# An inverse root moved from VectorE to ScalarE, and one chunk's VectorE order written out by itself

## The chip, the core and the metric

The program runs on one core of a Trainium2 chip. TensorE (PE) multiplies matrices, VectorE (DVE) and ScalarE (ACT) work element by element, GpSimd (POOL) does element-wise work on SBUF, and SyncE (SP) issues the transfers. Each engine takes its own instructions in the order in which they are written and waits at semaphores for the others. The metric is the device time of one execution in microseconds (us); lower is better.

## The reference

One layer of a hybrid encoder on 1,024 tokens of width 1,024, all in float32. What matters here is the second of its three token mixers (the SSD mixer) and the gated feed-forward part:

```python
# SSD mixer, after its scan: a gated norm over two groups of 192 channels
hg = (y.reshape(b_, s_, SSD_WIDTH) * jax.nn.silu(z.astype(jnp.float32)))
hg = hg.reshape(b_, s_, SSD_GROUPS, SSD_WIDTH // SSD_GROUPS)
hg = hg * lax.rsqrt(jnp.mean(jnp.square(hg), axis=-1, keepdims=True) + RMS_EPS)
ssd_out = (hg.reshape(b_, s_, SSD_WIDTH) * norm_w).astype(xbc.dtype)
...
mix = jnp.concatenate([pool_out, ssd_out, sb_out], axis=-1) @ w_out[i]
x = layer_norm(DEEPNORM_ALPHA * x + mix, ln1_g[i], ln1_b[i])
...
# feed-forward: up projection, causal convolution of width 3, gate, down projection
up = causal_depthwise_conv(x @ w_up, conv_w, conv_b)
gate, val = up[..., :D_FF], up[..., D_FF:]
ffn = (jax.nn.silu(gate) * val) @ w_down
```

## The kernel before, in words

**Numbers in two parts.** Every float32 matrix product is made as three matmuls on a high and a low part of each operand (`three`: high by high, high by low, low by high). ScalarE makes the high part by a rounding copy (`hi` for a whole weight unit of 128x1024, `op_hi` for a half of 128x512), VectorE the low part by a subtraction of the high part (`lo`, `op_lo`). A unit arrives by a transfer into one of two raw buffers; SP issues the transfer of a unit only when the low part of the unit two places earlier is made, since both share a buffer.

**The output projection.** The eight row blocks of `w_out` (units `("out", k)`) are taken in the order `OUT_ORDER = [5, 6, 7, 0, 1, 3, 2, 4]`. Blocks 2, 3 and 4 multiply the SSD mixer's result. TensorE sums the squares of the gated result (task `rm0`), then multiplies blocks 5, 6, 7, 0 and 1 for the first two token tiles, then spreads the inverse root over the partitions by two small products (tasks `sp0` and `sp2`, which read `tmp`), and then multiplies blocks 3, 2 and 4, each as 12 matmuls for the two token tiles. For each of these three blocks VectorE scales the mixer's tile (`normalised(k)`), ScalarE copies it to its high part, VectorE makes the low part of the weight block (`lo`) and then that of the tile (`mix_lo(k)`), and TensorE waits for that. In the kernel before, ScalarE makes the high part of a weight block ahead of the copy of the same step. The inverse root itself is: mean plus epsilon on VectorE, `Sqrt` on ScalarE, two reciprocals of half a tile on VectorE.

**The up projection.** It runs in 11 chunks of two column pairs; a pair (c, pp) is computed by a seven-product scheme after Strassen, with products named `A11, S1, S2, S3, A12, S4, A22` in TensorE's order, each of 12 matmuls. The operands `S1` to `S4` are sums of weight quarters that GpSimd makes in `weight_sums`; it can start when both raw buffers of the pair have arrived. The transfer into the second of them (`raw_b`) is issued by SP when VectorE has made the low part of `A22` of the pair before, and GpSimd's third sum waits for VectorE's low part of `S1`. VectorE adds products up in five steps, `combine(c, pp, 1)` to `combine(c, pp, 5)`; TensorE's `S4` product waits for step 2 and its `A22` product for step 3. VectorE also makes the convolution (`taps`), the gate product (`glu`) and the low part of the result (`h_low`), for whose high part ScalarE copies (`h_high`).

VectorE's order is written by hand: `first_chunk` for the first half of chunk 0 and `second_half(0)` for its second half, `chunk(c)` for the others, which calls `second_half(c)` too. After chunk 0 follow steps 1 and 2 of `combine(1, 0, ...)`.

Of the kernel before, what the change touches and what calls it, by code (L numbers as in the profile page):

```python
# [23 lines left out]
ALU = mybir.AluOpType  # L24
ACT = mybir.ActivationFunctionType

P = 128
D = 1024
S = 1024
HALF = 512  # L30
# [4 lines left out]
SSD_W = 384  # L35
# [11 lines left out]
RMS_EPS = 1e-6  # L47
# [24 lines left out]
OUT_ORDER = [5, 6, 7, 0, 1, 3, 2, 4]  # L72
# [5 lines left out]
UNIT = {u: n for n, u in enumerate(UNITS)}  # L78
# [215 lines left out]
def build(nc, ctx, a, out):  # L294
# [4 lines left out]
    def put(name, shape, dt=F32, at=None):  # L299

        size = -(-4 * int(np.prod(shape[1:])) // 32) * 32
        if at is None:
            at = top[0]
            top[0] += size
        assert at + size <= 229368, (name, at, size)
        return nc.alloc_sbuf_tensor_at(name, shape, dt, offset=at)

    def sem(name):
        return ctx.enter_context(nc.semaphore(name))
# [7 lines left out]
    un_b = put("weights_t1", [P, HALF], F32, top[0] - 4 * HALF)  # L317
    mask_r = put("mask", [P, P], F32R)
    zero = put("zero", [P, 1])
    cap_gt = put("cap_gt", [P, P])  # L320
    ident_r = put("ident_r", [P, P], F32R)
    pool_w = put("pool_w", [P, 2, P])
# [125 lines left out]
    xdt_done = sem("xdt_done")  # L448
    xw_done = sem("xw_done")
    hg_done, sq_done, nrm_done = sem("hg_done"), sem("sq_done"), sem("nrm_done")  # L450
    var_done, sqrt_done = sem("var_done"), sem("sqrt_done")
    rms_done = sem("rms_done")
    mixh = sem("mix_hi_done")
    ssd_split = sem("ssd_split")
# [64 lines left out]
    def hi(n):  # L519

        if UNITS[n][0] == "x":
            nc.scalar.wait_ge(x_raw[UNITS[n][1]], 16)
        else:
            nc.scalar.wait_ge(raw_in[raw_place(n) % RAWS], 16 * (raw_place(n) // RAWS + 1))
        wait_ring_free(nc.scalar, n)
        nc.scalar.activation(unit_place(n, False), unit_raw(n), ACT.Copy).then_inc(hi_done, 1)

    def lo(n, eng=nc.vector):

        eng.wait_ge(hi_done, n + 1)  # L530
        eng.tensor_tensor(unit_place(n, True), unit_raw(n), unit_place(n, False).bitcast(F32),
                                ALU.subtract).then_inc(split_done, 1)
# [66 lines left out]
    def op_lo(c, o, pp, it=0):  # L599

        nc.vector.wait_ge(op_hi_done, lo_count(c, o, pp) + 18 * it)
        nc.vector.tensor_tensor(op_place(c, o, pp, True), op_raw(c, o, pp), op_place(c, o, pp, False).bitcast(F32),  # L602
                                ALU.subtract).then_inc(op_lo_done, 1)
# [634 lines left out]
    def _(eng):  # L1238
# [208 lines left out]
        pooled_high(1)  # L1447
        squared(2)
        hi(UNIT[("out", 7)])
        nc.scalar.preload_act_table(ACT.Sqrt)  # L1450
        for k in (0, 1):
            hi(UNIT[("out", k)])
        eng.wait_ge(var_done, 1)
        act(tmp[:, :], tmp[:, :], ACT.Sqrt).then_inc(sqrt_done, 1)
        for k, unit in enumerate(OUT_ORDER[5:]):
            hi(UNIT[("out", unit)])
            i = (1, 0, 2)[k]
            eng.wait_ge(nrm_done, k + 1)
            act(mh[:, 2 + i, :], cv[:, i, :], ACT.Copy).then_inc(mixh, 1)


        def gain_bias(m):
# [171 lines left out]
    def _(eng):  # L1634
# [3 lines left out]
        def link(ins):  # L1638

            chained[0] += 1  # L1640
            ins.then_inc(dve_chain, 1)
            eng.wait_ge(dve_chain, chained[0])
# [33 lines left out]


        link(v.memset(zero[:, :], 0.0))
        for i, (n, s_) in enumerate(FIRST):
            if i < 3:  # L1680
                eng.wait_ge(first_hi, i + 1)
            else:
                eng.wait_ge(hi_done, 2)
            ins = v.tensor_tensor(unit_place(n, True)[:, s_], unit_raw(n)[:, s_], unit_place(n, False)[:, s_].bitcast(F32),  # L1684
                                  ALU.subtract)
            if i < 3:
                ins.then_inc(first_lo, 1)
            else:
                ins.then_inc(split_done, 2)
# [69 lines left out]
        def task(name):  # L1759
            eng.wait_ge(d_full, TASKS.index(name) + 1)  # L1760
            pair = task_place(name)[0]
            return two(pair), d_free[pair]
# [69 lines left out]
        def normalised(k):  # L1832
            i = (1, 0, 2)[k]
            src = task("sp%d" % i)[0] if k else tmp[:, :]
            v.scalar_tensor_tensor(out=cv[:, i, :], in0=cv[:, i, :], scalar=param("norm_w", i), in1=src,
                                   op0=ALU.mult, op1=ALU.mult).then_inc(nrm_done, 1)
# [5 lines left out]
                            ALU.subtract).then_inc(ssd_split, 1)  # L1842

        lo(UNIT[("out", 0)])
        src, free = task("rm0")
        v.tensor_scalar(tmp[:, :], src, 1.0 / (SSD_W // 2), RMS_EPS, ALU.mult, ALU.add).then_inc(var_done, 1)
        lo(UNIT[("out", 1)])
        eng.wait_ge(sqrt_done, 1)
        for h in range(2):
            s_ = slice(h * HALF, (h + 1) * HALF)  # L1850
            v.reciprocal(tmp[:, s_], tmp[:, s_]).then_inc(rms_done, 1)
        eng.wait_ge(rms_done, 2)
        normalised(0)
        lo(UNIT[("out", OUT_ORDER[5])])
        mix_lo(0)
        normalised(1)
# [72 lines left out]
        def taps(c, pp, r, it=0, parts=(1, 2)):  # L1929

            t = 2 * pp + r
            src = up_row(pp, r)
            w = PARAMS["ff_w"] + 3 * (4 * c + t)
            if 1 in parts:
                eng.wait_ge(row_tap, 4 * c + t + 1 + 4 * it)
                v.scalar_tensor_tensor(out=cf[:, r, 1:], in0=src[:, :S - 1], scalar=column(w + 1, 12, it),  # L1936
                                       in1=cf[:, r, 1:], op0=ALU.mult, op1=ALU.add).then_inc(row_mid, 1)
            if 2 in parts:
                eng.wait_ge(row_mid, 4 * c + t + 1 + 4 * it)
                v.scalar_tensor_tensor(out=cf[:, r, 2:], in0=src[:, :S - 2], scalar=column(w, 12, it),  # L1940
                                       in1=cf[:, r, 2:], op0=ALU.mult, op1=ALU.add).then_inc(row_done, 1)

        def glu(c, pp, it=0):

            eng.wait_ge(silu_ff, 2 * c + pp + 1 + 2 * it)
            eng.wait_ge(row_done, 4 * c + 2 * pp + 2 + 4 * it)
            v.tensor_tensor(cf[:, 0, :], cf[:, 0, :], cf[:, 1, :], ALU.mult).then_inc(glu_done, 1)
# [49 lines left out]
        def first_chunk():  # L1997

            combine(0, 0, 1)
            combine(0, 0, 2)  # L2000
            for i in range(2):
                eng.wait_ge(t_hi, 14 + 2 * i)
                v.tensor_tensor(t4l[:, 2 * i:2 * i + 2, :], sum_4[i][:, :, :], t4h[:, 2 * i:2 * i + 2, :].bitcast(F32),
                                ALU.subtract).then_inc(t_lo, 2)
            combine(0, 0, 3)
            op_lo(0, A22, 0)
            op_lo(0, A11, 1)
            combine(0, 0, 4)
            taps(0, 0, 0, 0, (1,))
            op_lo(0, S1, 1)  # L2010
            taps(0, 0, 0, 0, (2,))
            op_lo(0, S2, 1)
            op_lo(0, S3, 1)
            op_lo(0, A12, 1)
            combine(0, 0, 5)
            op_lo(0, S4, 1)

        def second_half(c, it=0):

            taps(c, 0, 1, it)  # L2020
            op_lo(c, A22, 1, it)
            glu(c, 0, it)
            h_low(c, 0, it)
            op_lo(c + 1, A11, 0, it)
            combine(c, 1, 1, it)
            combine(c, 1, 2, it)
            op_lo(c + 1, S1, 0, it)
            combine(c, 1, 3, it)
            op_lo(c + 1, S2, 0, it)
            op_lo(c + 1, S3, 0, it)  # L2030
            combine(c, 1, 4, it)
            op_lo(c + 1, A12, 0, it)
            taps(c, 1, 0, it)
            combine(c, 1, 5, it)
            op_lo(c + 1, S4, 0, it)
            taps(c, 1, 1, it)
            if c + 1 < LASTC:
                op_lo(c + 1, D0A, 0, it)
            glu(c, 1, it)
            if c + 1 < LASTC:  # L2040
                op_lo(c + 1, D1A, 0, it)
            h_low(c, 1, it)

        def chunk(c, it=0):

            combine(c, 0, 1, it)
            combine(c, 0, 2, it)
            op_lo(c, D0B, 0, it)
            combine(c, 0, 3, it)
            op_lo(c, D1B, 0, it)  # L2050
            op_lo(c, A22, 0, it)
            combine(c, 0, 4, it)
            taps(c, 0, 0, it)
            add_down(c, range(5), it)
            op_lo(c, A11, 1, it)
            add_down(c, range(5, 8), it)
            op_lo(c, S1, 1, it)
            op_lo(c, S2, 1, it)
            add_down(c, range(8, 16), it)
            op_lo(c, S3, 1, it)  # L2060
            op_lo(c, A12, 1, it)
            combine(c, 0, 5, it)
            op_lo(c, S4, 1, it)
            second_half(c, it)

        first_chunk()
# [282 lines left out]
```

## Time and profile before

| what | value |
|---|---|
| median of 3 executions | 1308.34 us (1306.91 to 1311.1) |
| the profiled execution, its own time | 1305.79 us |
| its span, first to last instruction | 1304.0 us |
| TensorE busy | 1278.3 us (98%) |
| VectorE, ScalarE, GpSimd busy | 65%, 39%, 18% |
| mean granted TensorE clock | 0.997 |

Times in the rows below count from the first instruction of the profiled execution. An engine's busy time says little by itself; what decides is where TensorE stands idle, and for whom it then waits.

### The profile page before, as it was taken

To read this page: it belongs to the slowest core of one execution; us is meant where nothing else is said; L and a number is where in the kernel's file an instruction comes from. 1 tells how busy PE (TensorE), PEld (TensorE's weight loads), DVE (VectorE), ACT (ScalarE), POOL (GpSimd) and SP (SyncE) were. 2 spreads that over 40 slices of the span, in tenths; PEclk is the share of its full clock that TensorE was granted. 3 is DMA by queue.
4 is the path that set the end of the run, shared out by engine and by line. 5 is a ranking of instruction groups with operands and counts; after the bars stand their busy time and mean duration, and the time that the engine had idled before them with its cause. 6 is when DMAs were issued, how large, how long until landed. Compare 5 with 4: busy or idle time off the path is not lost.

```text
span 1304.0 us, 16439 instructions
## 1 busy us (share of the span) xinstructions
PE 1278.3 (98%) x6120; PEld 1013.1 (78%) x6120; DVE 847.0 (65%) x1006; ACT 513.2 (39%) x792; POOL 232.7 (18%) x157
## 2 busy tenths in 40 slices
PE   7999999999999999999899999999999999999997
PEld 6777777777876888888788787878787787888886
DVE  5546646646498447525777676768676768677864
ACT  5435545457664126113434242423242323233441
POOL 0000000062300003510311111111111121212117
PEclk9999999999999999999999999999999999999999
DMA  6101101000004122100121111111121102011113
GB/s 239 50 32 38 40 21 49 32 34 17 1 17 145 50 81 81 58 24 23 59 65 49 49 49 48 64 32 64 48 66 47 64 32 64 32 65 33 59 60 124
DMA packets 22804, 71.94 MB, mean 55 GB/s; under 512 B 2528, under 2 KB 2784, under 8 KB 22752
## 3 DMA queue, kind: packets, MB, share of 16 engines
q1 hardware_dynamic: 22752, 71.22, 15.9%
q8 instruction: 36, 0.59, 0.2%
q14 instruction: 16, 0.13, 0.0%
HBM read 67.02 MB, written 4.19 MB: 55 GB/s over the span
## 4 chain that ended last, share of the span: by engine, by line
PE 73%; DVE 9%; issue 2%; ACT 2%; DMA 2%; DVEq 0%; SPq 0%; ACTq 0%
PE ps L734 12%; PE ps L736 12%; PE ps L735 12%; PE ps L1093 9%; PE ps L1095 9%; PE ps L1094 9%; PE ps L812 1%; PE ps L829 1%; DVE conv_ff L1936 1%; PE ps L788 1%; ACT conv_ff L1513 1%; DMA down_raw<-u_down 1%; DVE w_lo L602 1%; PE ps L1131 1%; PE ps L1133 1%
## 5 line engine op out<-in xcount | busy, mean ns | idle before, releaser
L734 PE MATMUL ps<-x_hi,w_hi 128*128 128x512 f32 x336 | 140.0, 417 | 8.1 <-DVE x_lo L1684 7.1
L1093 PE MATMUL ps<-mix_hi,w_hi 128*128 128x512 f32 x352 | 140.0, 398 | 3.3 <-DVE partial L1967 3.3
L1095 PE MATMUL ps<-mix_hi,w_lo 128*128 128x512 f32 x352 | 139.9, 397 | 0.0
L1094 PE MATMUL ps<-mix_lo,w_hi 128*128 128x512 f32 x352 | 139.7, 397 | 0.0
L736 PE MATMUL ps<-x_hi,w_lo 128*128 128x512 f32 x336 | 133.2, 396 | 0.0
L735 PE MATMUL ps<-x_lo,w_hi 128*128 128x512 f32 x336 | 133.2, 396 | 0.0
L1988 DVE TENSOR_TENSOR acc<-acc,ps 128x512 f32<-128x512 f32 x144 | 96.0, 684 | 54.3 <-PE ps L736 53.3
L2241 POOL TENSOR_TENSOR weight_sums<-raw 128x512 f32<-128x512 f32 x22 | 32.1, 1457 | 483.2 <-DMA raw<-u_up 483.2
L734 PE MATMUL ps<-h_hi,w_hi 128*128 128x512 f32 x288 | 114.7, 398 | 1.5 <-DVE acc L1988 1.5
L736 PE MATMUL ps<-h_hi,w_lo 128*128 128x512 f32 x288 | 113.9, 396 | 0.0
L735 PE MATMUL ps<-h_lo,w_hi 128*128 128x512 f32 x288 | 113.9, 395 | 0.0
L597 ACT ACTIVATE w_hi<-weight_sums 128x512 fp32r<-128x512 f32 x44 | 27.8, 632 | 210.7 <-PE ps L736 161.9
L1094 PE MATMUL ps<-t_lo,w_hi 128*128 128x512 f32 x264 | 104.4, 396 | 0.0
L1095 PE MATMUL ps<-t_hi,w_lo 128*128 128x512 f32 x264 | 104.4, 396 | 0.0
L1093 PE MATMUL ps<-t_hi,w_hi 128*128 128x512 f32 x264 | 104.4, 395 | 0.0
L1513 ACT ACTIVATE conv_ff<-ps,params 128x1024 f32<-128x1024 f32 x44 | 53.0, 1205 | 90.7 <-DVE ps L1974 53.5
L1708 DVE TENSOR_TENSOR_SCAN ps<-ps,zero 128x1024 f32<-128x1024 f32 (+7 forms) x48 | 65.3, 1361 | 33.4 <-ACT ps L1297 33.3
L734 PEld LDWEIGHTS ps<-x_hi,w_hi 128*128 128x128 f32 x336 | 63.7, 189 | 24.3 <-DVE x_lo L1684 7.1
L1093 PEld LDWEIGHTS ps<-mix_hi,w_hi 128*128 128x128 f32 x352 | 66.5, 189 | 19.7 <-DVE partial L1967 3.7
L1094 PEld LDWEIGHTS ps<-mix_lo,w_hi 128*128 128x128 f32 x352 | 66.6, 189 | 16.1
L1095 PEld LDWEIGHTS ps<-mix_hi,w_lo 128*128 128x128 f32 x352 | 66.5, 189 | 16.1
L1936 DVE SCALAR_TENSOR_TENSOR conv_ff<-ps,params,conv_ff 128x1023 f32<-128x1023 f32 x44 | 56.4, 1281 | 33.0 <-ACT conv_ff L1513 32.9
(268 smaller groups left out, 2733.5 us busy)
## 6 DMA issues: line engine op xcount, KB each, us to landing
raw<-u_up SPq DMA_DIRECT2D x44, 512.0 KB, 3.3
raw<-u_in SPq DMA_DIRECT2D x22, 512.0 KB, 3.3
down_raw<-u_down SPq DMA_DIRECT2D x38, 256.0 KB, 2.8
x_stage<-u_x SPq DMA_DIRECT2D x8, 512.0 KB, 7.8
raw<-u_out SPq DMA_DIRECT2D x8, 512.0 KB, 3.3
x_nat<-x_nat SPq DMA_DIRECT2D x8, 512.0 KB, 3.2
raw<-u_gate SPq DMA_DIRECT2D x8, 512.0 KB, 3.2
out<-o_norm SPq DMA_DIRECT2D x7, 512.0 KB, 2.6
```

The costliest lines, as they stand in the source:

```text
L597: nc.scalar.activation(op_place(c, o, pp, False), op_raw(c, o, pp), ACT.Copy).then_inc(op_hi_done, 1)
L734: mm(dst, w_hi, x_hi, start=first, stop=False)
L735: mm(dst, w_hi, x_lo, start=False, stop=False)
L736: return mm(dst, w_lo, x_hi, start=False, stop=last)
L1093: mm(dst, w_h[:, k], t_h[:, kt, :], start=fresh and kt == 0, stop=False, skip_group_check=True)
L1094: mm(dst, w_h[:, k], t_l[:, kt, :], start=False, stop=False, skip_group_check=True)
L1095: last = mm(dst, w_l[:, k], t_h[:, kt, :], start=False, stop=kt == 3, skip_group_check=True)
L1513: act(cf[:, r, :], up_row(pp, r), ACT.Identity, scale=column(w, 12, it), bias=column(b, 4, it)).then_inc(row_tap, 1)
L1708: link(v.tensor_tensor_scan(z[:, ::-1], z[:, ::-1], zero[:, 0:1].broadcast_to([P, keys]), 1.0, ALU.mult, ALU.add))
L1936: v.scalar_tensor_tensor(out=cf[:, r, 1:], in0=src[:, :S - 1], scalar=column(w + 1, 12, it), in1=cf[:, r, 1:], op0=ALU.mult, op1=ALU.add). ...
L1988: v.tensor_tensor(dst, dst, ps[:, DOWN_BANKS[k % 4], :], ALU.add).then_inc(dn_added, 1)
L2241: g.tensor_tensor(t0[:, :], wb[:, 0:HALF], wb[:, HALF:D], ALU.add).then_inc(sum_done, 1)
```

## The change

The inverse root is computed on ScalarE, as the exponential of minus half a logarithm: one `Ln` of a whole tile that also takes the mean and the epsilon (a new constant tile), and two `Exp` of half a tile. VectorE's three instructions for it go, and so does the semaphore `sqrt_done`. The load of the square root's table comes after the two `Exp`. ScalarE makes the high parts of the weight blocks 3, 2 and 4 one place later: that of block 3 after the copy of step 0, that of block 2 after the copy of step 1, that of block 4 after the copy of step 2. VectorE makes the low part of block 1 after `normalised(0)`.

In the feed-forward part the nine calls at the head of `second_half` move out of it: into `chunk` as they were, and into `first_chunk` in another order, in which the first three steps of `combine(0, 1, ...)` come earlier and the low parts of `A22`, of the result and of the next pair's `A11` and `S1` later.

```diff
@@ -317,6 +317,7 @@
     un_b = put("weights_t1", [P, HALF], F32, top[0] - 4 * HALF)
     mask_r = put("mask", [P, P], F32R)
     zero = put("zero", [P, 1])
+    rms_eps = put("rms_eps", [P, 1])
     cap_gt = put("cap_gt", [P, P])
     ident_r = put("ident_r", [P, P], F32R)
     pool_w = put("pool_w", [P, 2, P])
@@ -448,7 +449,7 @@
     xdt_done = sem("xdt_done")
     xw_done = sem("xw_done")
     hg_done, sq_done, nrm_done = sem("hg_done"), sem("sq_done"), sem("nrm_done")
-    var_done, sqrt_done = sem("var_done"), sem("sqrt_done")
+    var_done = sem("var_done")
     rms_done = sem("rms_done")
     mixh = sem("mix_hi_done")
     ssd_split = sem("ssd_split")
@@ -1447,16 +1448,21 @@
         pooled_high(1)
         squared(2)
         hi(UNIT[("out", 7)])
+        src, _ = task("rm0")
+        act(tmp[:, :], src, ACT.Ln, scale=1.0 / (SSD_W // 2), bias=rms_eps[:, 0:1]).then_inc(var_done, 1)
+        eng.wait_ge(var_done, 1)
+        for s_ in HALVES:
+            act(tmp[:, s_], tmp[:, s_], ACT.Exp, scale=-0.5).then_inc(rms_done, 1)
         nc.scalar.preload_act_table(ACT.Sqrt)
-        for k in (0, 1):
-            hi(UNIT[("out", k)])
-        eng.wait_ge(var_done, 1)
-        act(tmp[:, :], tmp[:, :], ACT.Sqrt).then_inc(sqrt_done, 1)
+        hi(UNIT[("out", 0)])
+        hi(UNIT[("out", 1)])
         for k, unit in enumerate(OUT_ORDER[5:]):
-            hi(UNIT[("out", unit)])
+            if k:
+                hi(UNIT[("out", OUT_ORDER[4 + k])])
             i = (1, 0, 2)[k]
             eng.wait_ge(nrm_done, k + 1)
             act(mh[:, 2 + i, :], cv[:, i, :], ACT.Copy).then_inc(mixh, 1)
+        hi(UNIT[("out", OUT_ORDER[7])])
 
 
         def gain_bias(m):
@@ -1676,6 +1682,7 @@
 
 
         link(v.memset(zero[:, :], 0.0))
+        link(v.memset(rms_eps[:, :], RMS_EPS))
         for i, (n, s_) in enumerate(FIRST):
             if i < 3:
                 eng.wait_ge(first_hi, i + 1)
@@ -1842,15 +1849,9 @@
                             ALU.subtract).then_inc(ssd_split, 1)
 
         lo(UNIT[("out", 0)])
-        src, free = task("rm0")
-        v.tensor_scalar(tmp[:, :], src, 1.0 / (SSD_W // 2), RMS_EPS, ALU.mult, ALU.add).then_inc(var_done, 1)
-        lo(UNIT[("out", 1)])
-        eng.wait_ge(sqrt_done, 1)
-        for h in range(2):
-            s_ = slice(h * HALF, (h + 1) * HALF)
-            v.reciprocal(tmp[:, s_], tmp[:, s_]).then_inc(rms_done, 1)
         eng.wait_ge(rms_done, 2)
         normalised(0)
+        lo(UNIT[("out", 1)])
         lo(UNIT[("out", OUT_ORDER[5])])
         mix_lo(0)
         normalised(1)
@@ -2014,18 +2015,18 @@
             op_lo(0, A12, 1)
             combine(0, 0, 5)
             op_lo(0, S4, 1)
+            taps(0, 0, 1)
+            combine(0, 1, 1)
+            combine(0, 1, 2)
+            op_lo(0, A22, 1)
+            glu(0, 0)
+            combine(0, 1, 3)
+            h_low(0, 0)
+            op_lo(1, A11, 0)
+            op_lo(1, S1, 0)
 
         def second_half(c, it=0):
 
-            taps(c, 0, 1, it)
-            op_lo(c, A22, 1, it)
-            glu(c, 0, it)
-            h_low(c, 0, it)
-            op_lo(c + 1, A11, 0, it)
-            combine(c, 1, 1, it)
-            combine(c, 1, 2, it)
-            op_lo(c + 1, S1, 0, it)
-            combine(c, 1, 3, it)
             op_lo(c + 1, S2, 0, it)
             op_lo(c + 1, S3, 0, it)
             combine(c, 1, 4, it)
@@ -2061,6 +2062,15 @@
             op_lo(c, A12, 1, it)
             combine(c, 0, 5, it)
             op_lo(c, S4, 1, it)
+            taps(c, 0, 1, it)
+            op_lo(c, A22, 1, it)
+            glu(c, 0, it)
+            h_low(c, 0, it)
+            op_lo(c + 1, A11, 0, it)
+            combine(c, 1, 1, it)
+            combine(c, 1, 2, it)
+            op_lo(c + 1, S1, 0, it)
+            combine(c, 1, 3, it)
             second_half(c, it)
 
         first_chunk()
```

## Rows read from the trace of the kernel before

**Rows 1.** The page, busy time by engine: us, share of the span, instructions.

```profile
PE 1278.3 (98%) x6120; PEld 1013.1 (78%) x6120; DVE 847.0 (65%) x1006; ACT 513.2 (39%) x792; POOL 232.7 (18%) x157
```

**Rows 2.** Waits of TensorE: us in total, times, longest.

```profile
PE ps L1093 <- DVE partial L1967: 3.3, 1, 3.3
```

**Rows 3.** Timeline of TensorE, output projection: start, length, instruction, [idle before <- releaser].

```profile
399.73 0.39 PE L734 MATMUL ps<-wo_hi,mix_hi 128*128 128x512 f32 x1
...
405.18 3.76 PE L1007 MATMUL ps<-tmp,tables 128*128 128x512 f32 x8
...
409.87 0.47 PE L734 MATMUL ps<-wo_hi,mix_hi 128*128 128x512 f32 x1 [0.93 <-DVE mix_lo L1841]
...
413.41 0.47 PE L734 MATMUL ps<-wo_hi,mix_hi 128*128 128x512 f32 x1 [0.54 <-DVE mix_lo L1841]
...
416.95 0.47 PE L734 MATMUL ps<-wo_hi,mix_hi 128*128 128x512 f32 x1 [0.57 <-DVE mix_lo L1841]
```

**Rows 4.** Timeline of VectorE, the same stretch.

```profile
395.25 1.23 DVE L531 TENSOR_TENSOR wo_lo<-raw,wo_hi 128x1024 fp32r<-128x1024 f32 x1 [1.15 <-ACT wo_hi L526]
...
399.49 6.56 DVE L1851 RECIPROCAL tmp<-tmp 128x512 f32<-128x512 f32 x2
...
409.64 1.27 DVE L1835 SCALAR_TENSOR_TENSOR conv<-conv,params,ps 128x1024 f32<-128x1024 f32 x1
410.83 1.22 DVE L531 TENSOR_TENSOR wo_lo<-raw,wo_hi 128x1024 fp32r<-128x1024 f32 x1
412.04 1.23 DVE L1841 TENSOR_TENSOR mix_lo<-conv,mix_hi 128x1024 fp32r<-128x1024 f32 x1
```

**Rows 5.** Timeline of ScalarE, the same stretch.

```profile
392.87 1.28 ACT L1450 ACT_TABLE_LOAD   x1
394.16 1.06 ACT L526 ACTIVATE wo_hi<-raw 128x1024 fp32r<-128x1024 f32 x1
...
407.40 1.06 ACT L1459 ACTIVATE mix_hi<-conv 128x1024 fp32r<-128x1024 f32 x1 [6.46 <-DVE conv L1835]
408.36 1.04 ACT L526 ACTIVATE wo_hi<-raw 128x1024 fp32r<-128x1024 f32 x1
...
410.94 1.06 ACT L1459 ACTIVATE mix_hi<-conv 128x1024 fp32r<-128x1024 f32 x1 [1.54 <-DVE conv L1835]
```

**Rows 6.** Groups of ScalarE by shape: busy us, mean ns | idle before.

```profile
L1397 ACT ACTIVATE c_scaled<-ps 128x1024 f32<-128x1024 f32 x6 | 6.1, 1040 | 2.4 <-PE ps L978 1.6 <-PE ps L960 0.8
```

**Rows 7.** Timeline of ScalarE, where the mixer's step sizes are made.

```profile
307.05 1.28 ACT L1364 ACT_TABLE_LOAD   x1
```

**Rows 8.** Timeline of TensorE, first two up chunks.

```profile
641.05 0.50 PE L1093 MATMUL ps<-mix_hi,w_hi 128*128 128x512 f32 x1 [3.26 <-DVE partial L1967]
...
645.50 0.39 PE L1093 MATMUL ps<-t_hi,w_hi 128*128 128x512 f32 x1
...
662.29 0.40 PE L1093 MATMUL ps<-mix_hi,w_hi 128*128 128x512 f32 x1
```

**Rows 9.** Stretches: us, busy time of PE, PEld, DVE, ACT, POOL, granted clock, DMA share, GB/s.

```profile
642.00:643.00 1.00, 1.00 (x4) 0.79 (x3) 1.00 (x2) 0.63 (x1) 0.37 (x2) 0.50 0.00 0
```

**Rows 10.** Timeline of VectorE, first two up chunks.

```profile
634.84 0.68 DVE L602 TENSOR_TENSOR w_lo<-raw,w_hi 128x512 fp32r<-128x512 f32 x1
...
637.78 1.22 DVE L1953 TENSOR_TENSOR h_lo<-conv_ff,h_hi 128x1024 fp32r<-128x1024 f32 x1 [1.12 <-ACT h_hi L1528]
...
640.31 0.69 DVE L1967 TENSOR_TENSOR partial<-partial,ps 128x512 f32<-128x512 f32 x1
641.43 1.27 DVE L602 TENSOR_TENSOR w_lo<-weight_sums,w_hi 128x512 fp32r<-128x512 f32 x1 [0.43 <-ACT w_hi L597]
...
646.43 0.68 DVE L1972 TENSOR_TENSOR ps<-partial,ps 128x512 f32<-128x512 f32 x1
...
660.25 0.69 DVE L1967 TENSOR_TENSOR partial<-partial,ps 128x512 f32<-128x512 f32 x1
```

**Rows 11.** Timeline of GpSimd, first two up chunks.

```profile
638.91 1.82 POOL L2241 TENSOR_TENSOR weight_sums<-raw 128x512 f32<-128x512 f32 x1 [10.74 <-DMA raw<-u_up]
```

## The prediction

> **What bounds the kernel now.** Read the busy times first: TensorE is busy 98% of the span [rows 1], so a change can only win where TensorE stands still, and loses wherever it makes TensorE wait. Then read what TensorE waited for. Its longest wait after the start of the kernel is a single one of 3.3 us for `partial`, VectorE's sum in the first up chunk [rows 2]; the wait for `mix_lo` in the output projection comes as three short stops of 0.93, 0.54 and 0.57 us [rows 3]. The change touches both places, and nothing else in the span. Last, read the timelines of the engines around the two places; the rest of the text follows the chain of instructions there. Between the two, TensorE paces everything (no other wait comes near these), so that a shift at the first place is carried to the second whole.
>
> **First place: the inverse root.** What is removed looks large: two reciprocals of together 6.56 us on VectorE [rows 4]. But TensorE doesn't wait for them. It multiplies blocks 5 to 1 until 405.18 us and then spreads the root for 3.76 us [rows 3]; the reciprocals end at 406.05, when only the second half of the first product can still need them, and no idle time stands there. Taking them away gives VectorE time, not TensorE.
>
> What is added lies on ScalarE. `Ln` of a whole tile from PSUM: the nearest row is `Exp` of the same shape from PSUM, 1.04 us [rows 6]; the `Ln` has a bias per partition in addition, so I take 1.15. No row shows it; the bounds are 1.04 and 1.5. Two `Exp` of half a tile cost no more than that row together, so some 1.25 us with the wait in between. They start where the table load started, at 392.87, and the load of 1.28 us follows them [rows 5]. So the load ends at 392.87 + 1.25 + 1.15 + 1.28 = 396.55, and the high part of block 0 starts there and not at 394.16. VectorE's low part starts 1.09 us after the high part (395.25 less 394.16) [rows 4, 5] and takes 1.23: made at 398.9. TensorE wants it at 399.73 [rows 3]. The slack of 0.8 us covers it; if it goes, each microsecond more on ScalarE costs TensorE one. The new constant is one small VectorE instruction at the start of the kernel, where VectorE waits for its first data: nothing.
>
> Of the load the row shows 1.28 us and the next instruction 0.01 us behind it [rows 5]. The Trainium skill, page "ScalarE: Activation LUTs", section "What ACT_TABLE_LOAD costs", has a drain of about 1.38 us besides. By that page the low part would come at 400.3, and the sum would be 0.6 us higher; the row decides, and I add nothing.
>
> The costly part is the order. Before, a step of blocks 3, 2 and 4 repeats every 3.54 us (409.87 to 413.41) [rows 3]: `normalised`, low part of the weight block, `mix_lo`; ScalarE's high part of the weight block lies ahead of the copy and is ready. After it, that high part is queued on ScalarE behind the copy of the same step, the copy waits for `normalised`, and VectorE takes the low part of the block before `mix_lo`. So for blocks 2 and 4 all of it stands in one chain: `normalised` to copy 1.30 us (409.64 to 410.94), copy to high part 0.96 (407.40 to 408.36), high part to low part 1.09, low part to `mix_lo` 1.21 (410.83 to 412.04), `mix_lo` to the next `normalised` 1.14 (the 3.54 less 409.64 to 412.04) [rows 3 to 5]: 5.70 us a step.
>
> Step 0 is early now. Its only late part is the transfer of block 3, which is issued when block 0's low part is made (398.9), some 2 us later than before; it has until 408.9. So TensorE goes from the root's products straight into block 3 at 408.94, and the stop of 0.93 us goes. Step 1 reads the first root product, which ends after half of the 3.76 us, at 407.1: `normalised(1)` at 407.16, copy 408.46, high part 409.42, low part 410.51, `mix_lo` 411.72. TensorE starts a block 1.37 us after `mix_lo` starts (412.04 to 413.41) [rows 3, 4]: block 2 at 413.09, not 413.41. Step 2 follows 5.70 us behind, block 4 at 418.79, not 416.95 [rows 3]. Stops of some 1.1 and 2.7 us take the place of the three. **Cost: +1.85 us**, with bounds of +1.5 and +2.4. Behind it the first normalization, the transfers of the gate weights and TensorE all shift alike.
>
> **Second place: the first up chunk.** The stop of 3.26 us stands before `S4` of pair (0, 1), at 641.05; behind it the 12 matmuls take 4.45 us to 645.50, where a product of 12 takes 2.80 elsewhere (645.50 to 662.29 holds six) [rows 8]. In that time the granted clock is 0.50, which is 1.2 GHz and not 2.4 [rows 9]. The stop is thus worth 3.26 + 1.65 = 4.9 us.
>
> In the new order steps 1 and 2 of `combine(0, 1, ...)` come at 634.84, where the low part of `A22` stood, and are done at 636.3; TensorE reaches `S4` at 637.8 (641.05 less 3.26) and need not stop. `A22` (step 3 done at about 638.7) and the five products of pair (1, 0) follow, each 2.80 us: TensorE is at `S4` of pair (1, 0) at 637.8 + 7 x 2.80 = 657.4, where before it was at 662.29. That product waits for `combine(1, 0, 2)`, which VectorE did at 660.25 to 660.94 [rows 10]. So the question is what is late next: how much earlier does VectorE come there? Its work between is the same, and almost without a pause.
>
> It comes later. The low part of `A22` moves behind two sums, from 634.84 to 636.24: 1.40 us (two rows of 0.69) [rows 10]. SP's queue waits for it to issue the transfer into `raw_b`, and GpSimd starts the next pair's sums when that has landed: 638.91, 3.4 us after the low part's end [rows 11]. From there the chain is as it was: GpSimd's sum, ScalarE's high part, VectorE's low part of `S1` at 641.43, GpSimd's third sum that waits for it, the low part of `S3`, and only then `combine(0, 1, 4)` at 646.43 [rows 10]. VectorE paused 0.43 us for `S1` [rows 10], so this chain sets the time. Of its 1.40 us I give back 0.2, since GpSimd's row of 1.82 us stood beside VectorE work that now lies elsewhere. Everything behind `combine(0, 1, 4)` follows it: `combine(1, 0, 2)` ends near 662.1. Bounds: 1.40 later (662.35), or 1.5 earlier (659.4), if VectorE's two pauses of 1.12 and 0.43 us [rows 10] close and the chain doesn't hold it.
>
> So `S4` of pair (1, 0) starts at 662.2 and not at 662.29: **-0.1 us** from there on. TensorE has stood for 4.8 us before it, longer than the 3.26 us after which the clock was low, and I charge the same 1.65 us once more: **+1.65 us** (bounds 0 and 3). Behind it TensorE sets the pace again.
>
> **Sum:** +1.85 - 0.1 + 1.65 = +3.4 us. The profiled execution took 1305.79 us for a span of 1304.0; it would become 1309.2. It lies 2.55 us under the median, so on the median's scale I forecast 1308.34 + 3.4 = **1311.7 us**. What a measurement of this kernel can tell from no change is about 0.3%, 3.9 us; the forecast is within it, on the slow side.
>
> **The rivals.** *The clock falls in the mixer too.* The stop of 2.7 us before block 4 is nearer to 3.26 us, behind which the clock fell, than to the 0.93 us behind which it didn't. If it falls, 1.65 us more: +5.0 us, 1313.4, slower. It decides at the length of that stop: `Ln` doesn't matter for it, only the chain of 5.70 us.
>
> *`Ln` brings table loads.* Where the step sizes are made, `Exp`, `Ln` and `Exp` each took a load of 1.28 us, three in a row [rows 7]. If it is so here, two more loads, 2.57 us, go past the slack of 0.8: +1.8 us, +5.2 in all, 1313.5. Against it: the stretch is entered with a set loaded by name, and `Exp` in it shows no load. The Trainium skill, "ScalarE: Activation LUTs", section "Table sets: the hidden batching unit", says that this set holds both functions, one load; by that the rival falls.
>
> *VectorE closes its pauses.* `combine(1, 0, 2)` ends at 659.4: `S4` starts 2.8 us earlier than before after a stop of 2.0 us and the clock stays: 1.85 - 2.8 = -0.9 us, 1307.4.
>
> *The stop goes for good.* VectorE keeps up to 657.4, 4.9 us won: 1.85 - 4.9 = -3.05 us, 1305.3. Against it stands VectorE's chain, which would have to shrink by 3.5 us. With the mixer's stops gone as well (2.0 us), 6.9 won: 1301.4, faster.
>
> **Chances.** Forecast 0.46, with its own range 1309.5 to 1313; of it 0.12 lies over the bound of 3.9 us, since its clock term may be 3. Clock in the mixer 0.18. Table loads 0.08. Pauses closed 0.12. Stop gone for good 0.08, of it 0.02 over the bound by the spread of runs; all stops gone 0.08. Faster: 0.02 + 0.08 = 0.10. Slower: 0.12 + 0.18 + 0.08 = 0.38. Within 0.3%: 0.52. The range reaches from under the closed pauses to over the table loads, with a microsecond of spread at either end: 1306 to 1315. It leaves out the stop gone, wholly or partly, and little on the upper side.
>
> **What would show it.** Right: no table load between `Ln` and `Exp`; TensorE's stops at `L734` of nothing, about 1.1 and 2.7 us; no stop at `S4` of pair (0, 1) but one of more than 4 us, five products later, for the same `partial`; GpSimd's sum some 1.4 us later beside TensorE's earlier products. Wrong: the high part of block 2 ready ahead of its copy; the last `combine` before 660; a clock that stays at 1.00 behind the stop.

## The result, and the profile after

The kernel after takes **1299.78 us** (median of 6 executions, 1298.68 to 1300.27), beside 1308.16 us for the kernel before on the same chip: a ratio of 0.9936 with an interval of 0.9925 to 0.9947, 8.4 us faster. The forecast was 3.4 us slower. The profiled execution took 1299.85 us for a span of 1298.1.

The waits of TensorE in the kernel after (engine, tile and line, what it waited for, then us in total, times, and the longest):

```profile
PE ps L735 <- DVE x_lo L1691: 7.3, 1, 7.3
PE ps L1094 <- DVE partial L1968: 6.3, 8, 4.6
PE ps L735 <- DVE acc L1989: 5.1, 7, 0.9
PE ps L735 <- DVE mix_lo L1848: 4.1, 2, 2.6
PE ps L789 <- DVE weights L1718: 2.4, 4, 0.9
PE ps L1094 <- ACT partial L1543: 1.2, 1, 1.2
```

Where there was one wait of 3.3 us for `partial` [rows 2] there are eight of 6.3 us in sum, and the waits for `mix_lo` have doubled [rows 3]. By its waits this kernel is slower. The gain must be where TensorE works, and the page's busy line says so:

```profile
PE 1260.1 (97%) x6120; PEld 1013.9 (78%) x6120; DVE 839.7 (65%) x1004; ACT 512.9 (40%) x794; POOL 232.7 (18%) x157
```

TensorE runs as many instructions as before, with 18.2 us less busy time [rows 1]. The same stretch of the up projection, in the timeline of TensorE (start, duration), of the kernel before:

```profile
710.12 0.40 PE L1094 MATMUL ps<-mix_lo,w_hi 128*128 128x512 f32 x1
710.36 0.40 PE L1095 MATMUL ps<-mix_hi,w_lo 128*128 128x512 f32 x1
710.59 0.40 PE L1093 MATMUL ps<-mix_hi,w_hi 128*128 128x512 f32 x1
710.82 0.40 PE L1094 MATMUL ps<-mix_lo,w_hi 128*128 128x512 f32 x1
```

and of the kernel after:

```profile
710.28 0.39 PE L1094 MATMUL ps<-mix_hi,w_hi 128*128 128x512 f32 x1
710.51 0.39 PE L1095 MATMUL ps<-mix_lo,w_hi 128*128 128x512 f32 x1
710.74 0.39 PE L1096 MATMUL ps<-mix_hi,w_lo 128*128 128x512 f32 x1
710.96 0.39 PE L1094 MATMUL ps<-mix_hi,w_hi 128*128 128x512 f32 x1
```

From start to start it is 233 ns before (0.70 us for three) and 227 ns after (0.68 for three). Of thousands of matmuls nobody edited, each is 6 ns shorter. What the edit changed for them is one thing: `rms_eps` takes 32 bytes of each partition, and every buffer placed behind it lies 32 bytes further.

The two places of the forecast stand in the trace much as foreseen. ScalarE at the inverse root, in its timeline (in brackets, idle time before and what ended it):

```profile
390.86 1.10 ACT L1452 ACTIVATE tmp<-ps,rms_eps 128x1024 f32<-128x1024 f32 x1
391.99 1.15 ACT L1455 ACTIVATE tmp<-tmp 128x512 f32<-128x512 f32 x2
393.16 1.28 ACT L1456 ACT_TABLE_LOAD   x1
394.45 2.05 ACT L527 ACTIVATE wo_hi<-raw 128x1024 fp32r<-128x1024 f32 x2
```

`Ln` takes 1.10 us, the two `Exp` 1.15, no load stands between them, and block 0 follows the load without a pause. VectorE in the output projection:

```profile
408.59 1.23 DVE L532 TENSOR_TENSOR wo_lo<-raw,wo_hi 128x1024 fp32r<-128x1024 f32 x1 [2.08 <-ACT wo_hi L527]
409.73 1.22 DVE L1848 TENSOR_TENSOR mix_lo<-conv,mix_hi 128x1024 fp32r<-128x1024 f32 x1
410.87 1.27 DVE L1842 SCALAR_TENSOR_TENSOR conv<-conv,params,ps 128x1024 f32<-128x1024 f32 x1
414.22 1.22 DVE L532 TENSOR_TENSOR wo_lo<-raw,wo_hi 128x1024 fp32r<-128x1024 f32 x1 [2.07 <-ACT wo_hi L527]
415.36 1.22 DVE L1848 TENSOR_TENSOR mix_lo<-conv,mix_hi 128x1024 fp32r<-128x1024 f32 x1
```

VectorE stands idle for 2.07 us in each step, waiting for the high part that ScalarE now makes behind the copy; a step takes 5.63 us (409.73 to 415.36) against 3.54 before. TensorE's stops at both places:

```profile
411.10 0.47 PE L735 MATMUL ps<-wo_hi,mix_hi 128*128 128x512 f32 x1 [1.45 <-DVE mix_lo L1848]
416.72 0.47 PE L735 MATMUL ps<-wo_hi,mix_hi 128*128 128x512 f32 x1 [2.62 <-DVE mix_lo L1848]
...
653.56 0.50 PE L1094 MATMUL ps<-mix_hi,w_hi 128*128 128x512 f32 x1 [1.21 <-ACT partial L1543]
661.18 0.79 PE L1094 MATMUL ps<-mix_hi,w_hi 128*128 128x512 f32 x1 [4.57 <-DVE partial L1968]
661.77 0.63 PE L1095 MATMUL ps<-mix_lo,w_hi 128*128 128x512 f32 x1
```

The stop at `S4` of pair (0, 1) [rows 8] is gone; one of 4.57 us stands at `S4` of pair (1, 0) instead. Busy time and granted clock by stretch (after the counts: the clock, the DMA share, GB/s):

```profile
410.00:415.00 5.00, 3.00 (x12) 2.17 (x12) 2.93 (x3) 2.82 (x3) 0.00 (x0) 1.00 0.32 105
415.00:420.00 5.00, 3.28 (x10) 2.64 (x11) 4.00 (x5) 0.13 (x1) 0.00 (x0) 0.79 0.31 105
420.00:425.00 5.00, 5.00 (x21) 4.05 (x21) 4.63 (x8) 1.15 (x2) 0.00 (x0) 0.87 0.32 107
...
660.00:665.00 5.00, 3.82 (x9) 3.05 (x10) 3.51 (x6) 1.67 (x3) 0.00 (x0) 0.52 0.19 66
665.00:670.00 5.00, 5.00 (x19) 3.98 (x19) 1.99 (x3) 1.72 (x2) 0.00 (x0) 0.80 0.69 210
```

Behind both long stops the clock fell to its lower level, 1.2 GHz: seven matmuls from 418.01 on take 0.63 us each, and so do those from 661.77 on, where the clock is 0.52, as it was 0.50 behind the stop of before [rows 9].

### The profile page after: what moved, and what is told of

Same layout as the page of the kernel before. It is cut to its first block, busy times and chain, and to the rows that moved or that the text cites. A ratio compares the mean times of both kernels' runs of the same rounds, so it can differ in the third digit from the quotient of the medians.

```text
span 1298.1 us, 16439 instructions
## 1 busy us (share of the span) xinstructions
PE 1260.1 (97%) x6120; PEld 1013.9 (78%) x6120; DVE 839.7 (65%) x1004; ACT 512.9 (40%) x794; POOL 232.7 (18%) x157
## 4 chain that ended last, share of the span: by engine, by line
PE 54%; DVE 16%; issue 7%; ACT 5%; DMA 4%; POOL 2%; DVEq 1%; ACTq 0%; SPq 0%; POOLq 0%
PE ps L735 12%; PE ps L737 12%; PE ps L736 12%; DVE conv_ff L1937 4%; DVE w_lo L603 3%; DMA raw<-u_up 3%; ACT conv_ff L1519 2%; PE ps L1094 2%; PE ps L1096 2%; PE ps L1095 2%; ACT w_hi L598 2%; PE ps L813 1%; PE ps L830 1%; DMA down_raw<-u_down 1%; POOL weight_sums L2251 1%
```

## The experiments

**The theories.** *Layout:* the gain is the shift alone; the order and the inverse root cost what the prediction said. *Order:* the new order gives the gain, and the shorter intervals are a by-product. Within layout, two forms: an address that is good in itself, or two operands of a product that must stand well to each other.

**One line alone, and the change without the shift.** The first kernel is the kernel before with an unused tile:

```diff
     zero = put("zero", [P, 1])
+    put("pad", [P, 1])
     cap_gt = put("cap_gt", [P, P])
```

The second is the kernel after with the constant behind all other buffers, so that nothing is shifted:

```diff
-    rms_eps = put("rms_eps", [P, 1])
...
+    rms_eps = put("rms_eps", [P, 1], F32, slot0 + 28 * 4 * kb)
```

> The kernel before with 32 unused bytes behind the tile of zeros, so that every later buffer lies 32 bytes higher; all instructions and their order are as before. Layout theory: the interval between two matmuls of the up and down projections falls from 0.2333 to 0.2267 us as in the changed kernel, and the time to 1296 us (1294 to 1299), below the changed kernel, since the dearer order is not in it. Order theory (the gain comes from the moved instructions): no change, 1308 us within 1.

> The changed kernel with the constant tile put behind the last buffer, so that all other buffers lie where they lay before. Layout theory: the interval stays at 0.2333 us and the order costs what the prediction summed, with the clock falling in the mixer as well: 1311 to 1314 us. Order theory: 1299.8 us, as the changed kernel.

Measured: the tile alone 1295.74 us beside 1307.45, a ratio of 0.9908 (0.9894 to 0.9921), faster than the change itself. The change without the shift 1311.97 us, 1.0039 (1.0026 to 1.0053): slower. The order theory falls. The two effects add up within the spread of the runs: -11.7 and +4.5 make -7.2, beside -8.4 measured for both together.

TensorE's stops in the unshifted change:

```profile
414.55 0.47 PE L735 MATMUL ps<-wo_hi,mix_hi 128*128 128x512 f32 x1 [1.46 <-DVE mix_lo L1848]
420.17 0.47 PE L735 MATMUL ps<-wo_hi,mix_hi 128*128 128x512 f32 x1 [2.65 <-DVE mix_lo L1848]
...
665.40 0.80 PE L1094 MATMUL ps<-mix_hi,w_hi 128*128 128x512 f32 x1 [4.55 <-DVE partial L1968]
```

The lengths are those of the kernel after, at unshifted intervals. So the shift did nothing to these stops, and the stops nothing to the gain.

**Either place alone, unshifted.** The unshifted kernel with the feed-forward order of before (the mixer's change alone), and the kernel before with the new order in the first up chunk alone (no constant at all).

> The same, with the inverse root and its order alone; VectorE's order in the first chunk as before. Layout theory: 1.85 us for the stops and 1.65 us if the clock falls behind the stop before block 4: 1310 to 1312 us. Order theory, if the mixer brought the gain: below 1305 us.

> The kernel before with VectorE's new order in the first chunk alone. Layout theory: the stop moves five products on and the clock falls there, +1.5 us: 1309 to 1311 us. Order theory, if the chunk brought the gain: 1303 us, 4.9 us less.

Measured: 1311.3 us (1.0029, 1.0018 to 1.0039) and 1308.68 us (1.0012, 1.0003 to 1.0021), +3.9 and +1.2 us; the second lies just under the range expected. Both edits cost time; neither has a hidden gain. In the mixer's profile the granted clock behind the second stop was 0.68 between 420 and 425 us; in the run of both places it was 1.00 there, so that run met its range without the fall on which the range was built. The fall behind a stop of 2.65 us comes in some executions.

The stop that the new order removes is not of one length either. With the chunk's order of before it was 3.26 us in the kernel before, but here, in the run of the mixer alone:

```profile
645.21 0.79 PE L1094 MATMUL ps<-mix_hi,w_hi 128*128 128x512 f32 x1 [4.34 <-DVE partial L1968]
```

Of the kernels below with that order and the pace of before (233 ns), one shows 3.26 us (the mended mixer, unshifted) and four show 4.35 to 4.41 (tiles of 64, 160 and 224 bytes, and 32 bytes everywhere). The forecast took this length from one execution; why it differs was not tried.

**A shift by 64 bytes, by 32 everywhere, and both operands at 32.** In the kernel before, the ring of weight buffers lies at multiples of 512 bytes and everything behind the small constants 224 bytes past one. The three kernels take `put("pad", [P, 16])` in place of the tile; `put("pad", [P, 1])` ahead of the weight ring, which shifts both operands; and that with a second tile of 32 bytes behind `zero`.

> The kernel before with 64 unused bytes behind the tile of zeros instead of 32. If what counts is an address within 64 bytes, every buffer lies as before in that sense: interval 0.2333 us, 1307.5 us within 1. Rival: any shift of these buffers, or a distance in larger steps, does it: near 1296 us.

> The kernel before with 32 unused bytes ahead of the first buffer, so that all buffers lie 32 bytes higher, the ring of up weights (a multiple of 64 before) and the tokens (32 over one before) alike. If what counts is that the two operands of a matmul lie alike within 64 bytes: they still don't, 0.2333 us and 1307.5 us within 1. Rival, the moving operand (the tokens) alone has to begin at a multiple of 64: it does now, 0.2267 us and near 1296 us.

> As the run with all buffers 32 bytes higher, with 32 more bytes behind the tile of zeros: weights and tokens both lie 32 bytes over a multiple of 64. If the two have to lie alike: 0.2267 us and near 1296 us. Rival, the moving operand has to begin at a multiple of 64: 0.2333 us and 1307.5 us.

Measured: 1306.79 us (0.9995, 0.9986 to 1.0004), 1307.62 us (0.9996, 0.9987 to 1.0005) and 1295.22 us (0.9900, 0.9884 to 0.9915). The first two are the kernel before, the third is as fast as the single tile, with both operands where the fast kernel has neither. An address good in itself falls; the distance between the operands counts. I took it for likeness within 64 bytes.

**The order mended, on the shifted kernel.** ScalarE's high parts are made ahead of their use, VectorE's low part of block 2 ahead of the second `normalised`, and the low part of `A22` of pair (0, 1) ahead of the convolution:

```diff
-            if k:
-                hi(UNIT[("out", OUT_ORDER[4 + k])])
...
             act(mh[:, 2 + i, :], cv[:, i, :], ACT.Copy).then_inc(mixh, 1)
-        hi(UNIT[("out", OUT_ORDER[7])])
+            for u in ((5, 6), (7,), ())[k]:
+                hi(UNIT[("out", OUT_ORDER[u])])
...
+        lo(UNIT[("out", OUT_ORDER[6])])
         normalised(1)
-        lo(UNIT[("out", OUT_ORDER[6])])
...
             op_lo(0, S4, 1)
+            op_lo(0, A22, 1)
             taps(0, 0, 1)
             combine(0, 1, 1)
             combine(0, 1, 2)
-            op_lo(0, A22, 1)
```

> The changed kernel (with its 32 bytes) with the order mended at both places: high parts of the blocks 3 and 2 behind the first copy and of block 4 behind the second, VectorE's low part of block 2 ahead of the second scaling, and in the first chunk the low part of A22 ahead of the convolution taps, so that its transfer and GpSimd's sums come earlier. Theory: no stops before the blocks 3, 2 and 4 (4 us and the low clock go) and a stop of under 3 us in chunk 1: 1290 to 1294 us, below the padded kernel before (1295.7). Rival, that the order is worth nothing: 1299.8 us.

Measured: 1294.43 us (0.9896, 0.9880 to 0.9911), just over the range expected. In the mixer one stop of 0.54 us is left. In the up chunk the long stop is not mended:

```profile
654.31 0.79 PE L1094 MATMUL ps<-mix_hi,w_hi 128*128 128x512 f32 x1 [4.39 <-DVE partial L1967]
654.90 0.63 PE L1095 MATMUL ps<-mix_lo,w_hi 128*128 128x512 f32 x1
```

4.39 us for the same sum, where under 3 were expected, and the clock at its lower level behind it. An earlier low part of `A22` is not enough to keep VectorE ahead in this order.

**The mended mixer alone, unshifted and shifted.** The same edits in the mixer, with the up chunk's order of the kernel before.

> The kernel after, with three differences: the constant tile lies where it shifts no other buffer; the feed-forward part has the order of the kernel before; and in the mixer the high parts of blocks 2 and 4 are made ahead of their use (both behind the copies of steps 0 and 1) and the low part of block 2 ahead of the second normalised tile. So it differs from the kernel before by the logarithm and exponential with this order alone. If the logarithm and exponential are worth something once the order around them is right, the stops of TensorE at the blocks 3, 2 and 4 (0.93, 0.54 and 0.57 us before) fall to 0.5 us or less in sum, and the time is 1305.9 to 1306.9, 1.0 to 2.0 us under the kernel before. If the inverse root has no part in those stops, the time is the kernel before's within 0.5 us.

> The same kernel with the constant tile where the change puts it, so that all later buffers lie 32 bytes further. If layout and order add up, it is 1.0 to 2.0 us under the kernel before with the 32 byte tile alone (1295.7), 1293.7 to 1294.7, and 11.5 to 13 us under the unshifted one. If the gain of the layout is bounded by VectorE in the feed-forward part, this change in the mixer still counts in full, since the mixer's stops are waits for VectorE there and the feed-forward part begins earlier by as much. If what the mixer gives is given back later, the time stays at 1295.2 to 1296.

Measured: 1306.78 us unshifted (0.9999, 0.9990 to 1.0008) and **1292.78 us** shifted (0.9882, 0.9866 to 0.9898), which beats the kernels before and after and is the fastest of all, though its interval overlaps those of the tile alone and of the kernel mended at both places. Both expectations failed. Unshifted, the stops in the mixer fell from 2.0 to 0.5 us, but the median only by 0.4. Shifted, the time lies under its range, 3.0 us below the tile alone (1295.74), while the mixer's stops fell only from 1.9 to 1.1 us; most of the 3.0 has no cause in these traces. What the logarithm is worth in the mended order lies between nothing and 3 us and isn't settled; in the submitted order it cost.

**One stage moved by itself.** To pin the effect to the operands, three of the four buffers that the down projection streams are moved in that fastest kernel, by 32 bytes, and in two more kernels by 64 and 128:

```diff
-    hh = [over("h_hi%d" % i, [P, S], (25, 26)[i], F32R) for i in range(2)]
-    hl = [over("h_lo%d" % i, [P, S], (27, 10)[i], F32R) for i in range(2)]
+    hh = [put("h_hi%d" % i, [P, S], F32R, slot0 + 4 * kb * (25, 26)[i] + 32) for i in range(2)]
+    hl = [put("h_lo%d" % i, [P, S], F32R, slot0 + 4 * kb * (27, 10)[i] + (32, 0)[i]) for i in range(2)]
```

> The mended kernel with the shifting tile (1292.78 us), in which three of the four buffers that the down projection streams (both high parts and one of the two low parts of the gated result) lie 32 bytes further, so that they stand otherwise within 64 bytes than the weights they meet; everything else stays where it was. If the two operands of a product must lie alike, the rows of the down projection alone go back: the means of the two with the high part from 393 and 389 ns to some 396, the one with the low part, of which half are moved, from 389 to some 392, while those of the up projection stay at 389. That is 288 x 2.5 x 6.6 ns = 4.8 us of TensorE; a part of it goes into the waits for VectorE's sums (5.3 us), so the time is 1293.8 to 1297.6. If the gain came from something else than these operands (the up projection's sums, the transfers, the order), these rows stay and the time is 1292 to 1293.6.

> The same with 64 bytes in place of 32: the operands lie alike again. If likeness within 64 bytes is what counts, the rows of the down projection are 393, 389 and 389 ns and the time is that of the mended kernel, 1292 to 1293.6. If any move of these buffers costs, it is as the one before.

> The mended kernel with the three buffers of the down projection moved by 128 bytes in place of 32 or 64. If likeness within 128 bytes counts, the rows of the down projection go back to 393, 389 and 389 ns and the time to that of the mended kernel, 1292 to 1293.8 us. If it is within 256 bytes, or if any move apart from the fourth buffer costs, it is as the two others, rows of 393 to 397 ns and 1296 to 1298.5 us.

Measured: 1296.63, 1298.07 and 1297.72 us, all some 4 to 5 us over the fastest kernel. The groups by line show that the stage alone pays (after the bar: busy us and the mean ns of one). The fastest kernel, down projection (two groups) and up projection:

```profile
L736 PE MATMUL ps<-h_lo,w_hi 128*128 128x512 f32 x288 | 112.1, 389 | 0.0
L737 PE MATMUL ps<-h_hi,w_lo 128*128 128x512 f32 x288 | 112.1, 389 | 0.0
L1094 PE MATMUL ps<-t_hi,w_hi 128*128 128x512 f32 x264 | 102.9, 390 | 0.4 <-DVE ps L1970 0.4
```

with the three buffers 32 bytes further:

```profile
L736 PE MATMUL ps<-h_lo,w_hi 128*128 128x512 f32 x288 | 113.1, 393 | 0.0
L737 PE MATMUL ps<-h_hi,w_lo 128*128 128x512 f32 x288 | 113.6, 394 | 0.0
L1094 PE MATMUL ps<-t_hi,w_hi 128*128 128x512 f32 x264 | 102.9, 390 | 0.3 <-DVE ps L1970 0.3
```

and 64 bytes further:

```profile
L737 PE MATMUL ps<-h_hi,w_lo 128*128 128x512 f32 x288 | 113.2, 393 | 0.0
L1094 PE MATMUL ps<-t_hi,w_hi 128*128 128x512 f32 x264 | 103.2, 391 | 0.3 <-DVE ps L1970 0.3
```

The up projection stays where it was and the down projection slows down, by as much as expected for 32 bytes: the operands' addresses are the cause. But 64 and 128 bytes were expected to differ from 32, by one form of the theory or another, and they don't. Likeness within 64 bytes falls here.

**The distance, swept.** The kernel before with unused tiles of 96, 160, 224, 288 and 544 bytes behind `zero` (`[P, 24]`, `[P, 40]`, `[P, 56]`, `[P, 72]`, `[P, 136]`).

> The kernel before with an unused tile of 96 bytes where the change puts its constant, so that the streamed operands lie 320 bytes from the weights' address, in the remainder of 512. If the two must lie alike within 64 bytes, this is fast, as the tile of 32 bytes was: 1294 to 1298 us. If they must lie alike within 128 bytes or 256, it is as the kernel before, within 2 us.

> The same with a tile of 160 bytes, a distance of 384. If they must lie alike within 64 or 128 bytes, this is fast, 1294 to 1298 us; if within 256 bytes, it is as the kernel before, within 2 us.

> The kernel before with an unused tile of 224 bytes, a distance of 448 between the weights and the streamed operands. If whole multiples of 256 count alone, the intervals are 229 to 233 ns and the time 1298 to 1308 us, since 448 is 64 short of one, as 320 was 64 over one (1298.4). If multiples of 64 count, 227 ns and 1294 to 1297.

> A tile of 288 bytes, a distance of 512. If multiples of 256 count, intervals of 227 ns and a time of 1294 to 1297 us. If the distance of 256 was good for itself, slower than 1298.

> A tile of 544 bytes, a distance of 768. If multiples of 256 count, intervals of 227 ns and a time of 1294 to 1297 us. If the period is longer than 256 and 512, slower than 1298.

The distance is the address of the first streamed buffer (48,352 before) less that of the weight ring (10,240), without whole multiples of 1,024. The interval is worked out from the starts in the timelines: the mean from a product of a token sum's low part with a high weight part to the next one, over the 264 pairs of the up projection. A weight tile takes 512 bytes (128 columns of 4), so successive tiles lie at distances that differ by 512: the row at 768 repeats that at 256, and the row at 512 has the distances of the output projection.

| tile, bytes | distance | interval, ns | time, us | ratio |
|---|---|---|---|---|
| none (before) | 224 | 233.4 | 1308.16 | 1 |
| 32 | 256 | 226.8 | 1295.74 | 0.9908 |
| 64 | 288 | 233.4 | 1306.79 | 0.9995 |
| 96 | 320 | 229.2 | 1298.38 | 0.9930 |
| 160 | 384 | 232.9 | 1306.52 | 0.9990 |
| 224 | 448 | 233.4 | 1308.19 | 1.0005 |
| 288 | 512 | 226.9 | 1294.68 | 0.9907 |
| 544 | 768 | 226.5 | 1295.93 | 0.9915 |

All multiples of 256 that were tried are fast, 256, 512 and 768; the output projection, whose two operands lie a multiple of 512 apart in every layout, has 227 ns in all of these runs. Of the rest one, 64 past a multiple, is in between (its time of 1298.38 us fits neither of its two forecasts), and the others lie at 233 (the run of 224 bytes, at 1308.19 us, just over its range). So the rule that fits all these layouts, in which every product of a stage has the same distance, is: a matmul of 128x512 here starts every 227 ns when the two operands lie a multiple of 256 bytes apart, and every 229 to 233 ns otherwise. The input projection, whose weights lie in the same ring, bears it out: the same mean, from a product of a token tile's low part to the next, is 232.7 ns in the kernel before and 228.1 in the kernel after. Why 320 is better than 448, and what in the chip makes it so, stays open.

## Why the prediction was wrong

**The step that failed** is the last sentence on the inverse root: "The new constant is one small VectorE instruction at the start of the kernel, where VectorE waits for its first data: nothing." The instruction costs nothing, but the constant has an address. With it fell two sentences of the first paragraph: that the change touches both places "and nothing else in the span", and that it "can only win where TensorE stands still". Both take the matmuls' pace in the rows of before as given. It quickened by 6.3 to 6.6 ns a matmul in the up and down projections, from start to start. With the tile alone TensorE's busy time falls from 1278.3 us to that in this line of its page:

```profile
PE 1261.5 (97%) x6120; PEld 1014.6 (78%) x6120; DVE 846.4 (65%) x1006; ACT 512.7 (40%) x792; POOL 232.5 (18%) x157
```

Not all of it reaches the end, since VectorE then comes nearer to being the bound: waits for `acc` rise from 1.5 to 5.4 us, those for `partial` from 3.3 to 5.5 and for `weights` from 1.8 to 2.4. 16.8 less 6.7 is 10.1; the span shrinks by 9.5 (1304.0 to 1294.5).

**The sum for the rest was right in its working.** +3.4 us were forecast, and the change without the shift measured +4.5.

*The mixer.* Stops of about 1.1 and 2.7 us were forecast, 1.46 and 2.65 measured; the step 5.70, measured 5.63. The unshifted run began its mixer 1.65 us later than the kernel before, ahead of any edit (a wait for `h_tiles` ends at 327.33 instead of 325.68 us). That is no cost of the new constant's instruction: with the unused tile of 224 bytes, which has no such instruction, the wait ends at 327.25. Counted from there, block 4 starts 92.84 us on, where before it was 91.27 (416.95 less 325.68): +1.57, for a forecast of +1.85.

*`Ln` and the tables.* 1.10 us for an estimate of 1.15, and no load between the functions, so the rival of the table loads fell, as the row of `Exp` without a load spoke against it.

*The chunk.* The stop moved and didn't go: 4.55 us for a forecast of 4.8, at the product named. Counted from the same point as above it lies at 338.07 us against 336.61, +1.46, where the mixer's +1.85 less 0.1 gives +1.75. GpSimd's sum comes 1.4 us later beside TensorE's earlier products, as foreseen (643.51 less 638.91, of which 1.65 and 1.57 are the late start and the mixer).

*The clock.* It fell behind the moved stop in every profile that has that stop, as charged. The rival that it falls in the mixer too came true in the kernel after and in the run of the mixer alone, and not in the run of both unshifted: it comes in some executions. With its 1.65 us the forecast for the mixer alone, +1.85, becomes +3.5, beside +3.9 measured.

*The rivals on the fast side* (pauses closed, stop gone) name mechanisms that didn't happen. The time fell below them all for a reason that wasn't among them.

Of what the prediction named as evidence that it was wrong, nothing showed: its chain of reasons could be confirmed line by line while the time went the other way. What would have caught it is the busy time of TensorE, read as a number that may change.

## What to carry to other kernels

A new buffer is two edits: what fills it, and what it does to the address of every buffer behind it; when TensorE is the bound, the second is worth checking first, with one unused tile of 32 bytes as the experiment. Place all streamed buffers of a main product a multiple of 256 bytes from its weights, and read the interval from start to start in the timeline: three matmuls in 0.68 us or in 0.70. When a time moves against all the waits, compare the busy time of the engine that bounds it before looking for another wait, and give a new constant a place that shifts nothing if an edit of order is to be judged by itself.

## What was unexpected of the hardware

The distance of two SBUF addresses changes the pace of these matmuls by 3% (226.8 or 233.4 ns). The Trainium skill, "TensorE: Matmul & The Clock Gate", section "Step-by-step: what each phase is for", says that the loading of the next weights and the streamed operand have read ports of their own, and that the load takes no read bandwidth from the running matmul. That alone gives no reason for an effect of their distance, and the runs show one: with three streamed buffers of the down projection 32 bytes further, its products grew from 389 to 394 ns while those of the up projection stayed at 390. Whether the load of the weights takes part in it isn't shown.

The moved buffers of one stage don't repeat the sweep exactly. At a distance of 320 the whole layout had 229 ns, while the down projection alone, moved to that distance, came to 233.0 ns from a low to the next high part. In that run one of the four buffers stayed at 256, so successive matmuls alternate between distances. The trace shows that this matters: the products that stream the unmoved buffer slowed down too, with a next start 230.8, 233.3 and 233.8 ns after theirs (moves of 32, 64 and 128 bytes), beside 226.8 in the fastest kernel. So the pace isn't set by a product's own two operands alone. Whether the next product counts by its streamed operand or by its weights, no run separates, since all weights lie alike.

The profiled execution of the run with the tile alone shows a granted clock of 0.945 for the whole span, while its intervals are 226.8 ns. It took 1296.28 us, amid the four others of the same kernel (1293.14 to 1297.87), whose clock reads 0.995 to 0.997. There a mean granted clock below 1.00 says nothing of the time.
